# Embedding tiles kept in the second-half columns of the slot table, router vector steps merged or moved, sample rows gathered as rounded part over rest

## The reference, cut to what matters

```
h = h + concat(c, r_out) @ w_out
h = h + hier_moe(rmsnorm(h, norm2_g), w_grp, b_grp, w_rt, b_rt, w_gate, w_up, w_down)
gate = sigmoid(rmsnorm(h, ple_norm_g) @ w_pg + b_pg)
h = h + gate * (p @ w_ple)
y = rmsnorm(h, final_g)
```

## Time and profile before

| | |
|---|---|
| median of 3 runs | 1426.43 us (1425.50 to 1427.19) |
| the profiled execution | 1425.37 us, span 1423.7 us |
| busy | PE 1334.0 us (94%), DVE 627.6 (44%), ACT 283.8 (20%), POOL 164.8 (12%) |
| chain that ended last | PE 55%, DMA 37%, ACT 2%, DVE 2% |
| HBM read | 481.06 MB, 342 GB/s over the span; 427 to 429 GB/s in most slices from the fourteenth of 40 on |

### The profile page before, as it was taken

One profiled execution on the slowest core, in us unless ns is written; L12 is line 12 of the kernel. 1 busy time (PEld: TensorE's weight loads), 2 busy tenths in 40 slices (PEclk: granted clock), 3 DMA queues, 4 the chain that ended last, 5 costly groups with the idle time before them and its releaser, 6 DMA issues.

```text
span 1423.7 us, 19742 instructions
## 1 busy us (share of the span) xinstructions
PE 1334.0 (94%) x8056; PEld 788.8 (55%) x8056; DVE 627.6 (44%) x1045; ACT 283.8 (20%) x409; POOL 164.8 (12%) x93
## 2 busy tenths in 40 slices
PE   8999999999799999999999999999999999998995
PEld 6999999999443333333333333333333333334995
DVE  7999786444433233223322223222332233225766
ACT  7334596333000000000000000000000000003653
POOL 1798600000000000000000000000000000001000
PEclk9999999999999999999999999999999999999998
DMA  9455445437699999999999999999999999999531
GB/s 348 160 208 180 151 147 208 148 142 291 237 387 402 428 429 428 428 429 428 429 428 429 428 429 429 428 428 429 428 429 428 429 428 427 429 428 413 192 135 62
DMA packets 44863, 486.30 MB, mean 342 GB/s; under 512 B 5201, under 2 KB 9329, under 8 KB 12033
## 3 DMA queue, kind: packets, MB, share of 16 engines
q1 hardware_dynamic: 41808, 481.35, 82.1%
q10 hardware_dynamic: 2688, 2.71, 0.6%
q0 software_dynamic: 320, 1.59, 0.3%
HBM read 481.06 MB, written 5.65 MB: 342 GB/s over the span
## 4 chain that ended last, share of the span: by engine, by line
PE 55%; DMA 37%; ACT 2%; DVE 2%; issue 1%; POOL 0%; SPq 0%; DVEq 0%; ACTq 0%
DMA ring<-in_w_exp_dram 36%; PE ps L929 17%; PE ps L955 6%; PE ps L760 4%; PE ps L764 4%; PE ps L761 4%; PE ps L724 4%; PE ps L708 4%; PE ps L715 4%; PE ps L966 3%; DVE hT L1782 1%; DMA embedding_rows<-ple_first 1%; PE ps L789 1%; DMA ring<-in_w_ple_dram 1%; PE ps L840 1%
## 5 line engine op out<-in xcount | busy, mean ns | idle before, releaser
L929 PE MATMUL ps<-ring,xwin 128*64 128x512 f32 x1984 | 452.4, 597 | 27.1 <-DMA ring<-in_w_exp_dram 22.6
L1782 DVE TENSOR_TENSOR hT<-hT,ps 128x1056 f32<-128x1056 f32 x128 | 160.4, 1254 | 363.5 <-PE ps L966 362.4
L929 PEld LDWEIGHTS ps<-ring,xwin 128*64 128x64 f32 x1984 | 149.2, 137 | 283.0 <-issue 213.8
L955 PE MATMUL ps<-ring,hid 128*64 128x512 f32 x1024 | 230.2, 603 | 16.4 <-DVE hid L1762 16.4
L955 PEld LDWEIGHTS ps<-ring,hid 128*64 128x64 f32 x1024 | 71.5, 138 | 151.5 <-issue 124.8
L966 PE MATMUL ps<-S,ysb 64*128 64x264 f32 x1024 | 148.3, 408 | 2.7 <-DVE hT L1782 1.8
L966 PEld LDWEIGHTS ps<-S,ysb 64*128 64x128 f32 x1024 | 88.4, 186 | 111.8 <-issue 101.5
L1278 ACT ACTIVATE sgl<-ps 64x512 f32<-64x512 f32 x32 | 18.8, 588 | 565.4 <-PE ps L929 565.4
L606 POOL COPY xwin<-xsT 128x1024 f32 x30 | 31.4, 1046 | 823.2 <-PE ps L929 823.2
L559 POOL TENSOR_TENSOR ring_r<-ring,ring_r 128x2048 fp32r<-128x2048 f32 x25 | 115.0, 4611 | 78.3 <-ACT ring_r L1098 78.3
L1098 ACT ACTIVATE ring_r<-ring 128x2048 fp32r<-128x2048 f32 x64 | 122.1, 1908 | 3.3 <-DMA ring<-in_w_in_dram 3.3
(11 more groups left out here) (305 smaller groups left out, 1300.7 us busy)
## 6 DMA issues: line engine op xcount, KB each, us to landing
ring<-in_w_exp_dram SPq DMA_DIRECT2D x192, 2048.0 KB, 25.1
ring<-in_w_in_dram SPq DMA_DIRECT2D x32, 1024.0 KB, 4.9
ring<-in_w_out_dram SPq DMA_DIRECT2D x16, 1024.0 KB, 4.7
ring<-in_w_pg_dram SPq DMA_DIRECT2D x16, 1024.0 KB, 5.2
hT<-in_x_dram SPq DMA_DIRECT2D x4, 528.0 KB, 4.9
pleT<-embedding_rows SPq DMA_DIRECT2D x1, 2112.0 KB, 25.9
out_y_dram<-hg SPq DMA_DIRECT2D x3, 528.0 KB, 2.9
ring<-in_w_ple_dram SPq DMA_DIRECT2D x2, 704.0 KB, 7.5
```

The source lines that it names most:

```text
L929: mm = pe.matmul(ps[part * WIN:(part + 1) * WIN, bank, :], window(k), weights(2 * j + part)[:, kk * F:(kk + 1) * F], start=(k == 0), stop= ...
L955: mm = pe.matmul(ps[half * WIN:(half + 1) * WIN, 2 + b, :], hid[:, t, :], weights(8 + t)[:, q * 512:(q + 1) * 512], start=(t == 0), stop=( ...
L1782: dve.tensor_tensor(group(hT, g), group(hT, g), ps[:, bank:bank + 4, 0:TOK].rearrange("p (h k) t -> p h k t", h=2), ALU.add)\
```

## The change

**Embedding tiles.** The eleven late tiles are copied by ACT into columns 264 to 527 of rows 0 to 3 and 5 to 11 of `xsT` (row 4 would lie on `iota`), and go to DRAM in three DMAs of 4, 3 and 4 tiles, each issued when its last tile is copied. The waits for `first_out` and `next_out` ahead of `take_slots(0)` and in POOL's pad step are gone; DVE waits for all three DMAs (`ple_out`) ahead of `take_slots(1)`. Those columns are written only by `take_slots(1)`.

**Sample rows.** DVE copies the 8 sample columns of each `hT` tile twice next to each other (`h_twice`), so that `turn_back` gives 16 rows at each of the four partition offsets; ACT copies them rounded with a sign (+1 in the first eight rows, -1 in the second), and DVE adds the unrounded value in the second eight rows, which leaves the rest there. `hp_few` and `hot_few` become one-pass operands with 16 rows, and `few_products` is four one-pass matmuls in place of four float32 ones. `spread_scale` uses the rounded part and the rest of the scale, two one-pass matmuls in place of one float32 matmul. The sign column is made from the identity by three short DVE steps at the start of the program.

**Router.** The weight table is widened from 36 to 40 columns, with a bias of -3.0e38 in the four spare ones, so that the copy into `gl` falls away; three `el` steps become one, two `ef` steps one, two `oh` steps one; the differences for the two softmaxes and `rest_hp(15)` move behind `asg`, and ACT's two exponentials behind the first scale copy. On PE, `token_squares` moves ahead of `logits(15)`.

```
         for m in range(KD):
             dve.wait_ge(acc_full, CT_OUT + m + 1)
...
             if m + 3 < KD:
                 rest_weights(W_IN + m + 3)
+            dve.wait_ge(h1_ready, m + 1)
+            dve.tensor_copy(h_twice[:, m % 2, :].rearrange("p (a t) -> p a t", a=2),
+                            hT[:, m, SEQ:TOK].unsqueeze(1).broadcast_to([P, 2, NB])).then_inc(twice_ready, 1)
             if m:
                 rest_hp(m - 1)
...
         def turn_back(m):
...
+            pe.wait_ge(twice_ready, m + 1)
             for kk in range(4):
-                pe.matmul(ps[32 * kk:32 * kk + NB, b, 2 * P:2 * P + 32], hT[:, m, SEQ:TOK],
+                pe.matmul(ps[32 * kk:32 * kk + 2 * NB, b, 2 * P:2 * P + 32],
+                          h_twice[:, m % 2, :],
...
-        logits(KD - 1)
-        pe.wait_ge(p_loaded, 16)
         pe.wait_ge(h1_summed, KD - 1)
         token_squares(ssq_full)
+        logits(KD - 1)
         turn_back(KD - 1)
+        pe.wait_ge(p_loaded, 16)
...
-                rows = slice(32 * kk, 32 * kk + NB)
+                rows = slice(32 * kk, 32 * kk + 2 * NB)
                 mm = pe.matmul(ps[:, gather_bank(i, kk), 0:TOK], hp_few[rows, j, :], hot_few[rows, cols],
...
-            pe.matmul(out, rstd[0:NB, 2:3].broadcast_to([NB, P]), hot_few[0:NB, cols], start=False, stop=True)\
+            pe.matmul(out, rstd_hi[0:NB, 2:3].broadcast_to([NB, P]), hot_few[0:NB, cols], start=False, stop=False)
+            pe.matmul(out, rstd_lo[0:NB, 2:3].broadcast_to([NB, P]), hot_few[0:NB, cols], start=False, stop=True)\
...
+            act.wait_ge(acc_full, CT_PLE + m + 1)
+            act.activation(xsT[:, PLE_ROWS[m], TOK:NSLOT], ps[:, (CT_PLE + m) % 3, 0:TOK], ACT.Copy).then_inc(ple_taken, 1)
+            for first, last in PLE_SPILLS:
+                if last == m + 1:
+                    act.wait_ge(ple_taken, last)
+                    act.dma_start(ple_dram[PLE_HEAD + first:PLE_HEAD + last].rearrange("m p t -> p m t"),
+                                  xsT[:, PLE_ROWS[first]:PLE_ROWS[last - 1] + 1, TOK:NSLOT]).then_inc(ple_out, 16)
...
+        dve.wait_ge(consts_ready, 5)
+        link(dve.tensor_reduce(ssum[:, 0:1], ident[:, :].rearrange("p (a b c) -> p b a c", b=2, c=NB)[:, 1, :, :],
+                               mybir.AxisListType.XY, ALU.add))
+        dve.tensor_copy(few_sign[:, 1:2], ssum[:, 0:1])
+        dve.tensor_scalar(few_sign[:, 0:1], ssum[:, 0:1], -2.0, 1.0, ALU.mult, ALU.add).then_inc(sign_ready, 1)
...
         def rest_hp(m):
...
+            few = hp_few[:, j, 32 * q:32 * q + 32]
+            stt(few, ps[:, 3 + m % 2, 2 * P:2 * P + 32], few_sign[:, 1:2], few.bitcast(F32), ALU.mult, ALU.add)
...
-        dve.wait_ge(first_out, 16)
         take_slots(0)
...
+        dve.wait_ge(ple_out, 16 * len(PLE_SPILLS))
         take_slots(1)
```

More of the change, by code:

```diff
@@ L185, in build @@
     onehot = place("onehot", [P, 2, NSLOT], F32R, r_free)
-    hot_few = place("hot_few", [P, NSLOT], F32, r_free + 4224)
+    hot_few = place("hot_few", [P, NSLOT], F32R, r_free + 4224)
     gbuf = place("gbuf", [P, 2, TOK], F32, r_free + 3168)
@@ L265, in build @@
     incl = rt("incl", [P, E])
+    h_twice = place("h_twice", [P, 2, 2 * NB], F32, ra + rsz[0])
+    ident_twice = place("ident_twice", [P, 2 * NB], F32, ra + rsz[0] + 128)
     over = rt("over", [P, E, 4])
@@ L341, in build @@
     few_cleared = sem("few_cleared")
+    twice_ready = sem("twice_ready")
+    sign_ready = sem("sign_ready")
     pos_ready = sem("pos_ready")
@@ L1256, in _ @@
         for m in range(PLE_FRONT):
[L1257 to L1268, removed]
-        act.dma_start(ple_dram[PLE_HEAD + PLE_FIRST:].rearrange("m p t -> p m t"), ple_next[:, :, :]).then_inc(next_out, 16)
+            act.wait_ge(acc_full, CT_PLE + m + 1)
[5 more added lines that the diff above has]
+                                  xsT[:, PLE_ROWS[first]:PLE_ROWS[last - 1] + 1, TOK:NSLOT]).then_inc(ple_out, 16)
         def keep_scale(half, bank):
@@ L1275, in _ @@
         keep_scale(0, 1)
+        act.wait_ge(softmax_in, 1)
+        act.activation(gex[:, :, :], gex[:, :, :], ACT.Exp)
+        act.activation(ex[:, :], ex[:, :], ACT.Exp).then_inc(softmax_out, 1)
         def silu_gate(sems, bank=0):
@@ L1645, in _ @@
                                gf[:, :].unsqueeze(2).broadcast_to([P, 3, NG]), ALU.is_equal))
-        for c in range(3):
-            last = dve.tensor_tensor(el[:, c, :, :], logit[:, c, NG:].rearrange("p (g j) -> p g j", g=NG),
-                                     oh4[:, c, :].unsqueeze(2).broadcast_to([P, NG, EG]), ALU.mult)
-        link(last)
+        link(dve.tensor_tensor(el[:, :, :, :], logit[:, :, GP:].rearrange("p c (g j) -> p c g j", g=NG),
+                               oh4[:, :, :].unsqueeze(3).broadcast_to([P, 3, NG, EG]), ALU.mult))
         link(dve.tensor_reduce(ein[:, :, :], el[:, :, :, :].rearrange("p c g j -> p c j g"), AX, ALU.add))
@@ L1670, in _ @@
         dve.tensor_tensor(rstd_lo[:, 0:3], rstd[:, 0:3], rstd_hi[:, 0:3].bitcast(F32), ALU.subtract)
+        rest_hp(KD - 1)
+        dve.tensor_tensor(ex[:, :], emx[:, :, 1], emx[:, :, 0], ALU.subtract)
+        dve.tensor_tensor(gex[:, :, :], logit[:, :, 0:NG], gmx[:, :, 0:1].broadcast_to([P, 3, NG]), ALU.subtract)\
+            .then_inc(softmax_in, 1)
         dve.wait_ge(ranks_full, 1)
@@ L1706, in take_slots @@
                 dve.wait_ge(slots_full, i + 1)
-                if half == 0 and k == 11:
-                    dve.wait_ge(next_out, 16)
                 if k == 0:
```

75 lines of the change are left out of this document (35 added, 40 removed).

## The result

The changed kernel takes 1419.71 us, the median of five runs (1418.36 to 1420.79), beside 1427.19 for the kernel before on the same chip: a ratio of 0.9937, with an interval from 0.9912 to 0.9963 (the two medians by themselves give 0.9948). It is faster, as forecast, but by less: the median lies 4.1 us above the forecast of 1415.6 and 0.7 above the upper end of the range. The kernel before ran 0.8 us slower here than the 1426.43 from which the forecast was made; against it 7.5 us are gained. The profiled execution took 1418.47 against 1425.37, so 6.9 us have to be found where 10.8 were forecast. Its page begins with

What follows compares the result with a forecast made beforehand. PE bounds it: its freeing of chunks in experts 0 and 1 moves the end one for one. Gains 8.50, 2.45, 2.30 less costs 1.45, 0.40, 0.20, 0.10, 0.30 give 10.8 us: 1415.6 from median 1426.43; range 1412.5 to 1419.0.

Steps and rivals of the forecast that it cites:

- the wait: First half's gather: without waiting for the first embedding transfer, expert 0 begins at 366.60 instead of 375.10; gain 8.50 us.
- sample rows and scale, first half: Gather before expert 0: cheaper one-pass products gain 0.55 a group, 0.45 for the scale, less 0.20 waiting for DVE; 2.45 us.
- the same, second half: Second half's gather: 0.45 for the scale, 3 x 0.55 for groups, 0.20 for the group in `gather_next`; gain 2.30 us.
- copy `h_twice`: First turn of the `w_out` loop: PE waits for the copy behind DVE's rest of a weight tile; cost 1.45 us.
- order on PE: End of `w_out`: `token_squares` waits for `acc`, a gap six logits products used to fill; cost 0.40 us.
- forty columns: Logits products: four more columns in 48 products of two pieces; cost 0.2 us taken, far end 1.2.
- sign column, start: Program start: three short DVE steps ahead of `states_ready`, nearly all swallowed by POOL's idle time; cost 0.10 us, between 0 and 0.4.
- key weights: PE's use of `S`: its transfer now meets expert 1's loads; cost 0.30 us, between 0 and 1.
- the starving rival: Late embedding transfers get only what loads leave, delaying the second half's slot tiles: 13 us lost, 1429.9; chance 0.04.
- the 55 KB/us: First embedding transfer's measured rate beside the loads, taken as a small but steady share; new transfers land by 375, costing nothing.
- run in turn: Rival for the gather's one-pass sample products: not side by side, about 0.35 us less in seven groups, 1418.0; chance 0.12.
- rival of a falling clock: Granted clock falls in PE's new 1.45 us wait at 239.7 us, costing 1.35 to 1.8: 1417.2; chance 0.14.

Runs made afterwards that it cites:

- e1: Kernel before with only the embedding-tile part of the change (new place, three transfers, later wait): 1419.97 us, ratio 0.9954.
- e8: Kernel before with only PE's new order at the end of `w_out`, token squares ahead of the last six logits products: 1426.32 us, ratio 1.0001.
- e2: Kernel before with only the sample rows part (`h_twice`, sign column, 16-row one-pass products, two scale products): 1429.22 us, ratio 1.0007.
- e6: Changed kernel with the doubled copy early, PE's old order, and the first sample products moved between the scale's products: 1416.15 us, ratio 0.9926.
- e10: Kernel of e6 plus extra PE products in the waits ending expert 1, and the fourth group's sample products first in their banks: 1415.97 us, ratio 0.9923.
- e3: Changed kernel with the doubled copy of the sample columns ahead of the rest of a weight tile on DVE: 1418.25 us, ratio 0.9934.
- e4: Changed kernel with PE's old order at the end of `w_out`, all last-turn logits products ahead of the token squares: 1419.57 us, ratio 0.995.
- e5: Changed kernel once more, unaltered, for a second profiled execution: 1421.84 us, ratio 0.9962.

## Why the prediction was right, and where it was wrong

The direction and the mechanism were right. The steps, forecast against measured in the profiled execution:

| step | forecast | measured | from |
|---|---|---|---|
| the wait | +8.50 | +8.57 | gather, before to e1 |
| sample rows and scale, first half | +2.45 | +1.54 | gather, e1 to after |
| the same, second half | +2.30 | +0.93 | 56.13 to 55.20, net of the wait for `S` |
| copy `h_twice` | -1.45 | -1.66 | PE's wait at 242 us |
| order on PE | -0.40 | -0.43 | e8's tail |
| clock behind it | 0 | -1.58 | 0.28 more in the tail, 1.30 in the seven tiles |
| forty columns | -0.20 | -0.09 | 99.94 to 100.03 |
| sign column, start | -0.10 | -0.69 | start; not the column (e2) |
| key weights | -0.30 | (0.27, inside the 0.93) | PE waits for `S` at 409.92 us |
| the end | 0 | +0.30 | behind expert 1 |
| sum | +10.8 | +6.9 | |

**The wait.** The step that carried the sum is confirmed by e1 alone to 0.07 us, with the restored clock in it (1.00 from 364 to 372 us, where it was 0.55 and 0.60). The transfers were out in time, so the starving rival falls, but not because of the 55 KB/us that spoke against it. That was a mean over a stretch in which the loads paused. In e1 the transfers moved 23 KB/us from 360 to 364 us, beside loads of 384 KB/us, about the 24 from which that rival decides; from 358 to 360 us, with the loads down to 200, they moved 171. When expert 0's loads ended at 366.3 us, 377 of the 1452 KB were left (440 were forecast), and they landed by 369.3 because expert 1's loads began only at 372.9. So the cost of nothing was right, and the steady share behind it was not; had the loads gone on at once, the rest would have landed near 383 us, by an estimate from the 23, some 4 us ahead of DVE's first slot tile at 387.3, where 10 us of cover were forecast.

The Trainium skill's rule of turns between queue rows, a packet each ("DMA: Bandwidth & Descriptors", section "Queues, rings and completion order"), agrees with this trace, where 89 packets of 1056 bytes passed from 360 to 364 us beside 96 of 16384.

**Sample rows: the term that was mis-sized.** The step that failed is to "add 0.14 for the change between float32 and one-pass work that falls away". The group went from 0.66 to 0.32 us, a gain of 0.33 a group where 0.55 was taken, because the gaps on both sides stayed: they come with the change between a 128-row and a 16-row stationary side, not with the number form, as e6 and e10 show by taking such changes away. The scale's two products, taken at 0.12 each, start 0.22 apart, which left 0.21 us (0.64 to 0.43) of the 0.45. In the first half 4 x 0.33 + 0.21 is the measured 1.54; the 0.20 us of waiting for DVE, which had been taken off, did not come. The rival "run in turn" is out all the same: the four products do run side by side.

**The order on PE: right by itself, wrong in what it may set off.** The rival of a falling clock was looked for behind the wait at 240 us, where it appeared in e2 and not in the changed kernel. There it came behind the wait of 0.38 us at 343, for which no rival was kept, and it alone is 1.58 of the 3.9 us that are missing. In both profiles with the two waits it fell there; with only the one for `acc` (e3, e8) or only the one for the copy (e2, e4) it did not. Nor is a wait needed for a fall: in e1 PE's rows show no idle time from 366 to 391 us, and the clock fell at 387.4, in products of 8 rows and of 64 columns. What links two waits 100 us apart, or whether six executions only fell so, stays open.

**Router steps, sign column, forty columns, key weights** were worth what was forecast or less. The 0.69 us at the start are the spread of executions, and most of that spread is one more fall of the clock: in six of the twelve profiles, kernels with and without the sign column among them, it fell near 22 us, and these come to the first turn at 241.09 to 241.57 us, the other six at 239.69 to 240.38, the copy's wait left out.

**The range** was built from terms and from the 0.9 us by which three runs spread to either side of their median. That was too few: the later runs of the kernel before spread over 2.9 us (13 runs), 3.1 (23) and 9.3 (17), the changed kernel's over 2.4 and 7. Part of it is that the clock falls at the end of expert 1 in some executions; the price, 861.2 to 862.6 us instead of 859.4 to 860.0 for the stage behind it, had no term. That these falls explain the whole spread is not shown, since only profiled executions show where the clock fell.

## What to carry to other kernels

When a long wait is taken out, price the short waits that the edit puts in as chances on a clock fall as well as by their length, and give a producer for the next engine its place ahead of long background work on its own engine: e6, with the copy early and the old order, beats both kernels at 1416.15 us. Before crediting a cheaper product between larger ones, look at the start-to-start gaps on both of its sides; what belongs to the change of shape stays when the product gets cheaper, and goes only when small products are put next to each other. And a transfer's mean rate over a stretch in which other traffic paused says little about its share while both run; count its packets where both do.

## What was not expected of the hardware

The clock fell behind waits as short as 0.38 us, and behind the same wait in some executions only: behind the copy's 1.6 to 1.7 us in one profile of four, behind `acc` in two of four, behind the 1.36 and 0.7 to 0.85 us at the end of expert 1 in four of ten. In e1 it fell with no wait ahead of it, so that the waits are its cause is not shown. It then stayed at 1.2 GHz for three to seven microseconds. A fall at the end of expert 1 costs more than PE's own loss, since chunks come free later and the loads start later (the DMA share is 0.35 and 0.17 behind it in the windows of e1 and e5); the changed kernel's two profiles, 1418.47 without such a fall and 1423.11 with one, differ by it more than by anything else (2.7 of 4.6 us, by the table of stages).
